# Attention scores on one Trainium2 core: the low part of the queries against 64 rows of the keys, two heads side by side

## The chip, the cores and the metric

The kernel is written instruction by instruction for one core of one Trainium2 chip. The metric is device microseconds of one execution; a run of the kernel is timed several times and the median is given. The engines of the core are TensorE (PE; its weight loads are listed as PEld), VectorE (DVE), ScalarE (ACT), GpSimd (POOL) and SyncE (SP, which here only issues DMAs). Each engine executes its own queue in order, and they wait for one another by semaphores.

## The reference, cut to what matters

One layer of a streaming encoder over 2048 prompt tokens and 32 tokens of a running stream with 1024 cached keys: a projection, a convolution group, an attention group, an output projection, and a mixture of experts. The change touches the scores of the attention group (8 heads of 64, query and key normalised, strictly causal, "stick-breaking" weights in place of a softmax):

```
z = einsum('bqhd,bkhd->bhqk', q, k) * 64 ** -0.5
valid = k_pos[None, :] < q_pos[:, None]
log_keep = where(valid, log_sigmoid(-z), 0.0)
later = cumsum(log_keep, axis=3, reverse=True) - log_keep
a = where(valid, exp(log_sigmoid(z) + later), 0.0)
o = einsum('bhqk,bkhd->bqhd', a, v)
```

## The kernel before, in words

The program has three phases with a barrier between them: `phase_project` (norm, input projection, convolution), `phase_attend` (attention, output projection, routing) and `phase_moe` (the experts). The change is in `phase_attend`.

**Precision.** The scores are made from parts. A query is split into an upper part `q_hi`, rounded to the matmul's fp32r type, and the remainder `q_lo`; a key likewise. A head has 64 dimensions and the array 128 rows, so the query parts lie twice in a tile, in rows 0 to 63 and again in rows 64 to 127 (`q_hi` and `q_lo`, each `[128, 2, 4, 128]`: two query tiles in turn, 4 heads of a group, 128 queries). The keys' tile `kt_sb` (`[128, 4, slots * 128]`) has for an even head the upper part in rows 0 to 63 and the lower in rows 64 to 127, and for an odd head the other way round. One matmul over all 128 rows thus gives the query part times upper plus lower key. A score needs two such passes, `q_hi` (line 1292) and `q_lo` (line 1296), summed in a bank of PSUM. So all four products of the parts are in it, lower query times lower key among them.

**Units.** Attention goes through 34 query tiles (two groups of 4 heads, 17 tiles of 128 queries each), and for each through pairs of heads and stretches of up to 4 key tiles of 128, from the latest keys back. One unit is one query tile, one pair of neighbouring heads (an even and an odd one) and one stretch: `attention_units` lists 172, of which 86 have 4 key tiles (512 columns), 70 have 3, 10 have 2 and 6 have 1. In a tile's first stretch, where the causal edge lies (68 units), a bf16 matmul of an identity with a mask adds -1e30 above the diagonal for each head (line 1294).

**Order on PE**, for each step s (the loop at the end of the function for `block.tensor`): `scores(s)`; jobs that `ahead(s)` names; `transpose_weights(s - 3)` (line 1304, up to 8 transposes of 128*128); the rest of the step's jobs; `values(s - 4)` (line 1321, up to 8 matmuls, which take 64 columns of the array per head, the even head into the lower and the odd into the upper half of the partitions of the output). The jobs are the transposes of keys and queries (lines 1230, 1235), the output projection in 12 matmuls of 512 columns (line 1256), transposes for the output and the router; a planner (`attention_jobs`) places up to two or three of them in a step, by due times and a cost count of columns.

**What scores feed.** For unit u ACT first makes `keep` of both heads (line 1413), a sigmoid of the negated scores, then `wgt` of both heads (line 1418), the sigmoid of the scores, both read from the scores' bank. DVE runs a product scan over `keep` for each head (line 1592, into `past`), POOL multiplies `wgt` by `past` (line 1709), PE transposes the result three steps later, ACT and DVE copy it out of PSUM (lines 1426 and 1604), and the values follow one step behind.

**Banks and waits.** Scores have 3 banks of 512 (`zp`), taken in turn, head by head: head number n = 2u + x uses bank n % 3. Before head n's first pass PE waits until `sig_done` tells that the second activation of head n - 3 has read the bank. After its last pass each head raises `z_done`, for which ACT's `keep` of that head waits. DVE also does the keys' and queries' lower parts (lines 1531, 1536) and the output projection's sum (line 1548).

Of the kernel before, what the change touches and what calls it, by code (L numbers as in the profile page):

```python
# [16 lines left out]
P = 128  # L17
# [4 lines left out]
NH, HD = 8, 64  # L22
# [738 lines left out]
def key_count(t):  # L761
    return t + 1 if t < PT else NPK


def key_slot(g, kt):

    if kt >= PT:
        return PT - NPK + kt - PT
    return PT + kt if g == 1 and kt < 4 else kt


def key_tiles(t, lo, hi):
    return [PT + a if t == PT else a for a in range(lo, hi)]
# [119 lines left out]
def phase_attend(nc, io, scr, picks):  # L893


    with ExitStack() as ctx:
        def sb(name, shape, dt=F32):
            return ctx.enter_context(nc.sbuf_tensor("p2_" + name, shape, dt))

        def ps(name, shape):  # L900
            return ctx.enter_context(nc.psum_tensor("p2_" + name, shape, F32))
# [3 lines left out]
        def sem(name):  # L905
            sems.append(nc.alloc_semaphore("p2_" + name))
            return sems[-1]
# [4 lines left out]
        NW, NK, NP, NA, NZ = 4, 2, 3, 4, 3  # L912
        HW = MAXU * P
        UW = PAIR * HW
        kt_sb = sb("kt", [P, HG, NS * P], F32R)
# [4 lines left out]
        q_lo = sb("q_lo", [P, 2, HG, P], F32R)  # L920
# [42 lines left out]
        zp = ps("zp", [P, NZ, 4 * P])  # L963
# [10 lines left out]
        z_done, keep_done, sig_done = sem("z_done"), sem("keep_done"), sem("sig_done")  # L974
# [65 lines left out]
        for u in range(len(units)):  # L1040
            s = u + 3
            w = (units[s][3] - units[s][2]) if s < len(units) else 0
# [20 lines left out]
        def width(u):  # L1063

            return (units[u][3] - units[u][2]) * P
# [133 lines left out]
        def _(pe):  # L1199
# [80 lines left out]
            def scores(u):  # L1280

                i, heads, lo, hi, _ = units[u]
                g, t = TILES[i]
                w, slot = width(u), key_slot(g, key_tiles(t, lo, hi)[0])
                pe.wait_ge(q_done, i + 1)
                pe.wait_ge(k_done, 2 * max(k_at[g, kt] for kt in key_tiles(t, lo, hi)) + 2)
                for x, h in enumerate(heads):
                    n = 2 * u + x
                    if n >= NZ:
                        pe.wait_ge(sig_done, n - NZ + 1)  # L1290
                    dst, mine = zp[:, n % NZ, 0:w], kt_sb[:, h, slot * P:slot * P + w]
                    pe.matmul(dst, q_hi[:, i % 2, h, :], mine, start=True, stop=False)
                    if hi == key_count(t):
                        pe.matmul(zp[:, n % NZ, w - P:w], identb[:, :], mask[:, :], start=False, stop=False,
                                  skip_group_check=True)
                    pe.matmul(dst, q_lo[:, i % 2, h, :], mine, start=False, stop=True).then_inc(z_done, 1)  # L1296

            def transpose_weights(u):
                pe.wait_ge(a_done, u + 1)
# [31 lines left out]
            for s in range(steps):  # L1331
                if s < len(units):
                    scores(s)
                for j in ahead(s):
                    job(j)
                if 0 <= s - 3 < len(units):
                    transpose_weights(s - 3)
                for j in behind(s):
                    job(j)
                if 0 <= s - 4 < len(units):  # L1340
                    values(s - 4)
# [885 lines left out]
```

## Time and profile before

| | |
|---|---|
| median of 3 runs | 2382.69 us (2379.04 to 2384.85) |
| the profiled execution | 2385.66 us, span of its instructions 2383.9 us |
| PE busy | 2175.3 us (91%) |
| PE weight loads (PEld) busy | 1809.6 us (76%) |
| DVE busy | 1823.2 us (76%) |
| ACT busy | 1336.5 us (56%) |
| POOL busy | 822.3 us (34%) |
| granted TensorE clock, mean | 0.962 of full |

Attention takes the stretch from about 549 to 1391 us of the span. A busy share counts the time in which at least one instruction of the engine was under way, and a matmul's record includes its way through the array: records of neighbouring matmuls overlap, so for the cost of one the starts of two neighbours are compared. "issue" as a releaser means that the engine stood idle while the profile shows nothing that it waited for.

### The profile page before, as it was taken

To read this page: it belongs to the slowest core of one execution; us is meant where nothing else is said; L and a number is where in the kernel's file an instruction comes from. 1 tells how busy PE (TensorE), PEld (TensorE's weight loads), DVE (VectorE), ACT (ScalarE), POOL (GpSimd) and SP (SyncE) were. 2 spreads that over 40 slices of the span, in tenths; PEclk is the share of its full clock that TensorE was granted. 3 is DMA by queue.
4 is the path that set the end of the run, shared out by engine and by line. 5 is a ranking of instruction groups with operands and counts; after the bars stand their busy time and mean duration, and the time that the engine had idled before them with its cause. 6 is when DMAs were issued, how large, how long until landed. Compare 5 with 4: busy or idle time off the path is not lost. (4 is left out here: it accounts for less than half of the span.)

```text
span 2383.9 us, 40219 instructions
## 1 busy us (share of the span) xinstructions
PE 2175.3 (91%) x13338; PEld 1809.6 (76%) x13339; DVE 1823.2 (76%) x2345; ACT 1336.5 (56%) x2487; POOL 822.3 (34%) x683
## 2 busy tenths in 40 slices
PE   8999999975989998899999774999999999999997
PEld 6888888854767776687777663888888888888886
DVE  4798999966888898878797856868688646656644
ACT  5223433345766677666666532667687646556633
POOL 0110664652666575555454430111111111111111
PEclk9999999996999999899999886999999999999999
DMA  6543243335332232333221115989899868768852
GB/s 220 194 144 112 97 133 115 112 104 165 103 101 92 68 129 76 86 106 118 80 76 63 45 47 207 359 286 369 290 371 373 275 216 270 256 189 278 278 181 44
DMA packets 210590, 407.03 MB, mean 171 GB/s; under 512 B 51967, under 2 KB 78463, under 8 KB 210461
## 3 DMA queue, kind: packets, MB, share of 16 engines
q1 hardware_dynamic: 196925, 356.11, 42.6%
q0 software_dynamic: 13536, 49.29, 8.9%
q8 instruction: 71, 1.16, 0.2%
q14 instruction: 58, 0.48, 0.1%
HBM read 312.66 MB, written 92.67 MB: 170 GB/s over the span
## 5 line engine op out<-in xcount | busy, mean ns | idle before, releaser
L2062 DVE TENSOR_TENSOR p_w_lo<-p_raw,p_w_hi 128x1024 fp32r<-128x1024 f32 x384 | 446.0, 1219 | 178.5 <-ACT p_w_hi L1864 174.9
L1709 POOL TENSOR_TENSOR p_wgt<-p_wgt,p_past 128x768 f32<-128x768 f32 (+3 forms) x172 | 335.0, 1948 | 362.5 <-DVE p_past L1592 358.4
L1864 ACT ACTIVATE p_w_hi<-p_raw 128x1024 fp32r<-128x1024 f32 x384 | 376.9, 1050 | 63.4 <-PE p_up L1950 51.8
L563 DVE SCALAR_TENSOR_TENSOR p_ut<-p_ut,p_cw 128x512 f32<-128x512 f32 (+1 forms) x480 | 347.8, 799 | 0.0
L1592 DVE TENSOR_TENSOR_SCAN p_past<-p_keep,p_past 128x513 f32<-128x513 f32 (+1 forms) x208 | 304.0, 1501 | 46.3 <-ACT p_keep L1413 45.0
L298 PE MATMUL p_pj<-p_w_hi,p_xt_hi 128*128 128x512 f32 x680 | 271.4, 399 | 7.0 <-DVE p_xt_lo L539 2.4
L298 PE MATMUL p_pj<-p_w_hi,p_xt_lo 128*128 128x512 f32 x680 | 266.7, 392 | 0.0
L298 PE MATMUL p_pj<-p_w_lo,p_xt_hi 128*128 128x512 f32 x680 | 266.1, 391 | 0.0
L1413 ACT ACTIVATE p_keep<-p_zp 128x384 f32<-128x384 f32 (+3 forms) x344 | 168.1, 542 | 134.8 <-PE p_zp L1296 126.9
L1950 PE MATMUL p_gp<-p_w_lo,p_xt_hi 128*128 128x256 f32 x736 | 206.8, 281 | 0.0
L1950 PE MATMUL p_gp<-p_w_hi,p_xt_lo 128*128 128x256 f32 x736 | 206.8, 281 | 0.0
L1950 PE MATMUL p_gp<-p_w_hi,p_xt_hi 128*128 128x256 f32 x736 | 206.7, 281 | 0.0
L1426 ACT ACTIVATE p_at<-p_tp 128x512 f32<-128x512 f32 (+3 forms) x281 | 142.3, 556 | 95.4 <-PE p_tp L1304 95.0
L1592 DVE TENSOR_TENSOR_SCAN p_past<-p_keep 128x385 f32<-128x385 f32 (+3 forms) x136 | 167.2, 1269 | 34.2 <-ACT p_keep L1413 33.5
L1304 PE MATMUL p_tp<-p_ident,p_wgt 128*128 128x128 f32 x1160 | 164.0, 280 | 17.1 <-DVE p_at L1604 16.3
L2136 POOL DMA_INDIRECT y_out<-p_yo,p_at_s x47 | 75.5, 1605 | 288.7 <-ACT p_yo L1893 288.5
L1939 PE MATMUL p_dp<-p_w_hi,p_ht_hi 128*128 128x512 f32 x368 | 152.9, 415 | 20.7 <-DVE p_ht_lo L2083 20.7
L1321 PE MATMUL p_op<-p_at,p_v 128*64 128x128 f32 x2320 | 168.5, 285 | 0.0
L1418 ACT ACTIVATE p_wgt<-p_zp 128x384 f32<-128x384 f32 (+3 forms) x344 | 167.1, 555 | 0.0
L1304 PEld LDWEIGHTS p_tp<-p_ident,p_wgt 128*128 128x128 f32 x1160 | 139.4, 145 | 31.2 <-DVE p_at L1604 20.1
L2124 POOL COPY p_at_g<-p_slots 128x1 int32 (+1 forms) x47 | 8.6, 184 | 445.4 <-PE p_xtp L1920 418.6
L298 PEld LDWEIGHTS p_pj<-p_w_hi,p_xt_hi 128*128 128x128 f32 x680 | 128.5, 189 | 34.4 <-DVE p_xt_lo L539 2.8
(253 smaller groups left out, 5014.4 us busy)
## 6 DMA issues: line engine op xcount, KB each, us to landing
p_raw<-in_w_up SPq DMA_DIRECT2D x128, 512.0 KB, 8.6
p_raw<-in_w_gate SPq DMA_DIRECT2D x128, 512.0 KB, 5.2
p_raw<-in_w_down SPq DMA_DIRECT2D x128, 512.0 KB, 7.1
p_w_raw<-in_w_in SPq DMA_DIRECT2D x40, 256.0 KB, 3.9
p_x<-in_x SPq DMA_DIRECT2D x17, 512.0 KB, 4.3
p_qd<-scr_q SPq DMA_DIRECT2D x68, 128.0 KB, 3.3
p_y<-in_x SPq DMA_DIRECT2D x17, 512.0 KB
scr_y<-p_y SPq DMA_DIRECT2D x17, 512.0 KB, 3.0
```

The source lines that it names most:

```text
L298: last = pe.matmul(pj[:, n % NPJ, :], xa[:, b, k, :], wa[:, place[c], k, :], start=(m == 0), stop=(m == 3 * KT - 1))
L563: dve.scalar_tensor_tensor(dst, src, cw[:, a, j:j + 1], dst, ALU.mult, ALU.add).then_inc(tap_done, 1)
L1304: end = pe.transpose(tp[:, x, b * P:(b + 1) * P], wgt[:, u % NW, x * HW + b * P:x * HW + (b + 1) * P], ident[:, :])
L1321: end = pe.matmul(op[x * HD:(x + 1) * HD, pair * P:(pair + 1) * P], v_sb[:, key_slot(g, kt), h * HD:(h + 1) * HD], at[:, (2 * u + x) % NA, ...
L1413: act.activation(keep_rows[:, u % NK, x, HW - w:HW], zp[:, (2 * u + x) % NZ, 0:w], ACT.Sigmoid, scale=-SCALE).then_inc(keep_done, 1)
L1418: act.activation(wgt[:, u % NW, x * HW:x * HW + w], zp[:, (2 * u + x) % NZ, 0:w], ACT.Sigmoid, scale=SCALE).then_inc(sig_done, 1)
L1592: end = dve.tensor_tensor_scan(past[:, u % NP, to + w + 1:to:-1], src, src, past[:, (u - 1) % NP, to + 1:to + 2] if more else 1.0, ALU.mul ...
L1709: pool.tensor_tensor(mine, mine, past_rows[:, u % NP, :, 2:2 + w], ALU.mult).then_inc(a_done, 1)
L1864: act.activation(w_hi[:, p, :], raw[:, n % RING, :], ACT.Copy).then_inc(whi_done, 1)
L1939: last = pe.matmul(dp[:, c, :], ha[:, f, :], wa[:, KT + f, c * 512:(c + 1) * 512], start=(start and n == 0), stop=(not start and n == 5))
L1950: last = pe.matmul(dst, xa[:, k, :], wa[:, piece, at + lo:at + hi], start=(n == 0), stop=(n == 3 * KT - 1))
L2062: dve.tensor_tensor(w_lo[:, p, :], raw[:, n % RING, :], w_hi[:, p, :].bitcast(F32), ALU.subtract).then_inc(wlo_done, 1)
```

## The change

The two `q_lo` passes of a unit leave the loop over the heads and follow in a loop of their own behind it. Each takes 64 rows in place of 128: rows 0 to 63 for the even head (x = 0), rows 64 to 127 for the odd one (x = 1), which are the rows with the upper part of that head's keys. The product of the lower query part with the lower key part is left out. The order on PE becomes q_hi of the first head, its mask if there is one, q_hi of the second head (behind its wait for the bank), its mask, q_lo of the first, q_lo of the second. Each q_lo still raises `z_done` once.

```diff
@@ -1293,7 +1293,11 @@
                     if hi == key_count(t):
                         pe.matmul(zp[:, n % NZ, w - P:w], identb[:, :], mask[:, :], start=False, stop=False,
                                   skip_group_check=True)
-                    pe.matmul(dst, q_lo[:, i % 2, h, :], mine, start=False, stop=True).then_inc(z_done, 1)
+                for x, h in enumerate(heads):
+
+                    rows = slice(x * HD, (x + 1) * HD)
+                    pe.matmul(zp[:, (2 * u + x) % NZ, 0:w], q_lo[rows, i % 2, h, :],
+                              kt_sb[rows, h, slot * P:slot * P + w], start=False, stop=True).then_inc(z_done, 1)
```

## Rows read from the trace of the kernel before

**Rows 1.** The score lines 1292 and 1294: count, duration min/median/max in ns, first and last start, shapes.
```profile
L1292 PE MATMUL p_zp<-p_kt,p_q_hi x344: 273/401/796, 548.9 to 1389.6; 128*128 128x512 f32 x86, 128*128 128x384 f32 x70, 128*128 128x256 f32 x10, 128*128 128x128 f32 x6
...
L1294 PE MATMUL p_zp<-p_mask,p_identb x136: 229/230/330, 549.1 to 1377.4; 128*128 128x128 bf16 x136
```
**Rows 2.** Busy time of each engine by stretch of attention, in us (number of instructions).
```profile
core 0: us, PE busy (x) PEld busy (x) DVE busy (x) ACT busy (x) POOL busy (x), PEclk, DMA share, GB/s
...
700.00:850.00 150.00, 138.95 (x1058) 110.23 (x1058) 130.02 (x112) 101.53 (x229) 93.06 (x65) 0.98 0.28 88
850.00:1000.00 150.00, 129.05 (x996) 100.62 (x995) 134.04 (x135) 106.24 (x246) 89.59 (x55) 0.95 0.32 98
...
sum 830.00, PE 749.63 PEld 598.62 DVE 701.34 ACT 558.46 POOL 462.02; mean PE 124.94 PEld 99.77 DVE 116.89 ACT 93.08 POOL 77.00
```
**Rows 3.** Waits, 560 to 1390 us: us in total, times, longest.
```profile
ACT p_keep L1413 <- PE p_zp L1296: 126.8, 100, 7.8
...
DVE p_past L1592 <- ACT p_keep L1413: 78.5, 60, 4.4
PEld p_op L1321 <- issue: 31.2, 158, 0.4
PEld p_zp L1292 <- issue: 29.4, 166, 0.3
...
PE p_tp L1304 <- DVE p_at L1604: 16.3, 10, 2.9
...
PE p_zp L1292 <- ACT p_wgt L1418: 3.4, 3, 1.7
```
**Rows 4.** Timeline of PE, 805.7 to 806.7 us: start, duration, instruction.
```profile
805.76 0.39 PE L1256 MATMUL p_mp<-p_wo_lo,p_m_hi 128*128 128x512 f32 x1
805.99 0.40 PE L1256 MATMUL p_mp<-p_wo_hi,p_m_lo 128*128 128x512 f32 x1
806.32 0.65 PE L1321 MATMUL p_op<-p_at,p_v 128*64 128x128 f32 x7
```
**Rows 5.** Timeline of PEld, 17.4 to 18.8 us (first phase).
```profile
17.91 0.32 PEld L306 LDWEIGHTS p_pm<-p_ident,p_sq 30*128 30x128 f32 x4 [0.17 <-issue]
```
**Rows 6.** Timeline of PE, 807.0 to 810.3 us: a unit of 384 columns without a mask.
```profile
807.35 0.45 PE L1292 MATMUL p_zp<-p_kt,p_q_hi 128*128 128x384 f32 x1
807.63 0.34 PE L1296 MATMUL p_zp<-p_kt,p_q_lo 128*128 128x384 f32 x1
807.80 0.35 PE L1292 MATMUL p_zp<-p_kt,p_q_hi 128*128 128x384 f32 x1
807.99 0.34 PE L1296 MATMUL p_zp<-p_kt,p_q_lo 128*128 128x384 f32 x1
808.16 1.04 PE L1304 MATMUL p_tp<-p_ident,p_wgt 128*128 128x128 f32 x8
809.13 1.09 PE L1321 MATMUL p_op<-p_at,p_v 128*64 128x128 f32 x16
```
**Rows 7.** Timeline of PEld, the same stretch.
```profile
807.99 0.97 PEld L1304 LDWEIGHTS p_tp<-p_ident,p_wgt 128*128 128x128 f32 x8
809.13 0.85 PEld L1321 LDWEIGHTS p_op<-p_at,p_v 128*64 128x64 f32 x16 [0.17 <-issue]
```
**Rows 8.** Timeline of PE, 1180.7 to 1182.2 us: a unit of 512 columns without a mask.
```profile
1181.11 0.50 PE L1292 MATMUL p_zp<-p_kt,p_q_hi 128*128 128x512 f32 x1
1181.44 0.39 PE L1296 MATMUL p_zp<-p_kt,p_q_lo 128*128 128x512 f32 x1
1181.67 0.40 PE L1292 MATMUL p_zp<-p_kt,p_q_hi 128*128 128x512 f32 x1
1181.90 0.40 PE L1296 MATMUL p_zp<-p_kt,p_q_lo 128*128 128x512 f32 x1
1182.14 0.27 PE L1304 MATMUL p_tp<-p_ident,p_wgt 128*128 128x128 f32 x1
```
**Rows 9.** Timeline of PE, 1190.3 to 1192.3 us: a unit of 512 columns with masks.
```profile
1190.61 0.50 PE L1292 MATMUL p_zp<-p_kt,p_q_hi 128*128 128x512 f32 x1
1190.96 0.23 PE L1294 MATMUL p_zp<-p_mask,p_identb 128*128 128x128 bf16 x1
...
1191.90 0.60 PE L1263 MATMUL p_mp<-p_ident,p_h 128*128 128x128 f32 x4
```

## The prediction

> **What bounds the kernel now.** Only the attention phase issues the edited lines, from 549 to 1390 us of the span [rows 1]. I read first the busy times by stretch, then the waits of that stretch, then single units on the timeline.
>
> The kernel's three phases follow one another, so time lost or won inside attention is not hidden by the others: the question is whether TensorE (PE) is what attention waits for. Over 560 to 1390 us PE is busy 749.63 of 830.00 us and VectorE (DVE) 701.34 [rows 2]. PE is thus without work for 80.4 us, a tenth: 11 of 150 us from 700 to 850, 21 from 850 to 1000. The waits say the same from the other side: DVE stands 78.5 us in front of its scan until ScalarE (ACT) has made the keep weights, in 60 pieces, and ACT's own wait for the scores is 126.8 us; PE's largest single wait, for a copy of DVE's, is 16.3 us [rows 3]. So attention is paced by PE nine tenths of the time, with DVE close behind.
>
> PE also has idle that no other engine causes: before the values' first weight load 158 times, 31.2 us, and before the scores' first one 166 times, 29.4 us, both put down to "issue", 0.18 to 0.20 us each [rows 3]. They stand where PE goes from full 128*128 matmuls to the 128*64 ones of the values, and back. After a full matmul of 512 columns the next full one begins 0.23 us later (805.76 to 805.99), but the values behind it 0.33 us later (805.99 to 806.32) [rows 4]. So at a change of the array's division the next weight load waits until the array is empty, 0.10 us over the pitch, and then is itself exposed. The four 30*30 matmuls of the first phase, which have fewer rows as well as fewer columns, show the same 0.17 us of held-back load [rows 5].
>
> The Trainium skill has this as a rule (TensorEngine Tiling (Array Packing), Key Properties): a change of tiling mode, not of tile alone, drains TensorE. Rows 3 to 5 agree for columns, and for rows and columns together; no row shows a change of rows alone.
>
> **The change, part by part.** (a) Each head's second pass (q_lo) takes 64 rows instead of 128. (b) The two q_lo passes of a unit move behind both q_hi passes, next to each other, one on the lower 64 rows, one on the upper. The number of instructions, the banks and the semaphore increments stay. They are moved on PE's queue alone, past nothing but the other head's q_hi and mask; no DMA, and nothing of SP or POOL. There are 172 units: 86 with 512 columns, 70 with 384, 10 with 256, 6 with 128 (two heads each, so 344 q_hi passes); 136 masks are 68 units [rows 1].
>
> *Fewer rows, by themselves: nothing.* Full passes cost by columns, 0.23 us at 512 [rows 4] and 0.17 to 0.19 at 384 [rows 6]; no row has 64 rows. I take no gain from (a) alone; only running side by side can give one.
>
> *Running side by side: likely.* The values of the two heads already do it in two column halves: 16 of them take 1.09 us, hardly more than 8 full transposes at 1.04 [rows 6], and their 16 weight loads take 0.85 against 0.97 for 8 [rows 7]. Two halves load and stream in one period. I take the same for row halves: the pair costs one pass. The bounds are one pass (0.23 us at 512) and two.
>
> *Two new changes of division in each unit* (128 rows to 64 and back), besides the two that are there. In an unmasked unit of 512 columns the first q_hi starts at 1181.11, the transposes behind the scores at 1182.14: 1.03 us in steps of 0.33, 0.23, 0.23, 0.24 [rows 8]; the first is 0.10 longer because its weight load is exposed. After the change: 0.33 to the second q_hi; 0.33 until the load of the low pair may start [rows 4]; 0.10 for that exposed load; 0.33 from the pair's stream to the next load; some 0.05 for the transposes' exposed load (half, since a transpose's pitch is about half of a 512 pass; an estimate). Sum 1.14: **0.11 us more** for each of 86 units, 9.5 us.
>
> At 384 columns the unit takes 807.35 to 808.16, 0.81 us [rows 6]. After: 0.28 + 0.28 + 0.10 + 0.28 + 0.05 = 0.99, where the drained steps are 0.33 less the 0.05 by which this pitch is shorter. **0.18 us more** for 70 units, 12.6 us: the saved pass is worth less here and the drains cost the same. The 16 smaller units I put at 0.2 us, 3.2 us. A masked 512 unit takes 1.29 us (1190.61 to 1191.90) [rows 9]; each mask stays behind its q_hi. By the same sum it comes out 0.02 us better than an unmasked one, which I neglect. **PE: 9.5 + 12.6 + 3.2 = 25 us more.**
>
> Bounds of the unknown: without any drain at a change of rows, the pair saves one pitch in each unit, 86 x 0.23 + 86 x 0.18 = 35 us less. With drains and no overlap it is 25 + 35 = 60 us more. With drains and overlap of streams alone, the loads one after the other, it is 172 x 0.10 = 17 us over the forecast. I take 25, since the column halves are the nearest row.
>
> *The moved q_lo delays the first head's scores.* They end now 0.33 + 0.39 = 0.72 us after the first q_hi starts [rows 8]; then 0.33 + 0.33 + 0.10 + 0.39 = 1.15. The second head's end stays (0.33 + 0.23 + 0.23 + 0.40 = 1.19 before). So the first keep activation and the first scan of a unit come 0.43 us later wherever ACT and DVE stand waiting: 60 times, 26 us of more DVE idle at most. PE's being three units ahead of the transposes that need the result hides it, and DVE has 830 - 701 = 129 us without work; with that cover gone it would cost up to those 26 us. I count 0, and it widens the range upward. Also, the second q_hi waits for the bank that the previous unit's activation frees, and now the first q_lo, then the transposes and values, stand behind it. Waits of this kind are 3.4 us now [rows 3]; I add as much again, 3 us.
>
> **Sum.** Of 25 + 3 us nine tenths are on the path (PE is without work a tenth of the time, and takes up delays there): 25 us, less about 2 for stretches where DVE is behind anyway: 23 us. The profiled execution took 2385.66 us (span 2383.9), 3 us over the median of 2382.69; so 2383 + 23 = **2406 us**, 1.0% slower.
>
> The Trainium skill also has a rule that promises a gain (TensorE: Matmul & The Clock Gate, Part 3): matmuls in different row groups run at once, their starts some 4 ns apart. Taken alone it would give the 35 us less of the bounds; no run shows row halves yet.
>
> **The rivals.**
> 1. *No drain for row halves* (faster). The halves' weights load behind the running q_hi, as those of full passes do. For: the column side of the array does not change, and all drained cases in the trace change it. Against: these are all the changes of division there are, and each is drained. Price: 35 us less of PE; DVE (701 us busy) then becomes the bound more often and lets perhaps 0.7 through: 25 us less, **2358**. It decides once the low pair starts less than about 0.25 us behind the second q_hi.
> 2. *Drains, no overlap*: 60 us of PE, nine tenths through, **2438**. For: nothing in the trace shows two row halves at once. Against: rows 6 and 7. That the change does not do what it says lies here too: the passes would run one after the other as full ones do.
> 3. *Small drains, or absorbed*: each drain costs about half of its 0.10; then a 512 unit gains 0.01 and a 384 one 0.08, 6 to 7 us in all; or PE's tenth of idle and DVE's pace take up most of the 25: **2386**.
>
> **How the numbers follow.** Forecast 0.47, rival 1 0.19, rival 2 0.14, rival 3 0.20. A difference of 0.3%, 7 us, is about what a measurement of this kernel can tell from none; 0.17 of rival 3 lies within it, 0.02 above, 0.01 below. Faster 0.19 + 0.01 = 0.20, same 0.17, slower 0.47 + 0.14 + 0.02 = 0.63. Given the forecast alone, 2394 to 2424 (0.07 to 0.24 us a unit). The range reaches from near rival 1 to rival 2, 2362 to 2440, and leaves out about half of the first and a third of the second.
>
> **What would show it.** Right: in a 512 unit the first low pass starts 0.3 us or more behind the second q_hi, with an "issue" idle before its load, and the second low pass within some 0.01 us of the first; the load behind the pair also shows "issue" idle, and these waits grow by some 60 us in total (344 x 0.17); attention ends about 23 us later, and the expert phase keeps its length. Wrong: no new "issue" waits and a low pair that follows in 0.23 us (rival 1); low passes a full pass apart (rival 2); PE's added time there, but its waits for DVE smaller by as much (rival 3).

## The result, and the profile after

The changed kernel takes 2407.3 us (median of 5 runs, 2401.62 to 2411.56) against 2382.69 us before: ratio 1.0099, 95% interval 1.0074 to 1.0124, 24.6 us or 1.0% slower. The forecast was 2406. The profiled execution took 2402.61 us, 5 us under the median; that of before 3 us over its own, so the two traces lie 17 us apart.

The scores' lines in the changed kernel, with the columns of [rows 1]; the idle in front of them and who waited for them:
```profile
L1299 PEld LDWEIGHTS p_zp<-p_kt,p_q_lo x344: 182/183/288, 546.5 to 1406.5; 64*128 64x128 f32 x172
L1299 PE MATMUL p_zp<-p_kt,p_q_lo x344: 322/491/795, 546.5 to 1406.5; 64*128 64x512 f32 x86, 64*128 64x384 f32 x70, 64*128 64x256 f32 x10, 64*128 64x128 f32 x6
...
  issue: 35.4, 104
who waited for it (us, times):
  ACT p_keep L1417: 172.1, 114
```
The scores run from 545.5 us (line 1292's first) to 1406.5, 861 us against 841 before; from the last scores to the end it is 994 us in both. The whole difference lies in attention.

One unit of 512 columns on PE's timeline (739.1 to 740.8 us), then one of 384 (615.8 to 617.1):
```profile
739.28 0.73 PE L1292 MATMUL p_zp<-p_kt,p_q_hi 128*128 128x512 f32 x2
739.95 0.49 PE L1299 MATMUL p_zp<-p_kt,p_q_lo 64*128 64x512 f32 x2
740.37 0.65 PE L1308 MATMUL p_tp<-p_ident,p_wgt 128*128 128x128 f32 x4
...
615.91 0.62 PE L1292 MATMUL p_zp<-p_kt,p_q_hi 128*128 128x384 f32 x2
616.45 0.44 PE L1299 MATMUL p_zp<-p_kt,p_q_lo 64*128 64x384 f32 x2
616.82 0.55 PE L1308 MATMUL p_tp<-p_ident,p_wgt 128*128 128x128 f32 x3
```
The two low passes take 0.49 us together; each alone would be 0.49 as well (0.39 plus the exposed load), so they run at the same time. (A matmul's record begins with its own exposed load: 0.50 us instead of 0.40.) The pair starts 0.67 us behind the first q_hi (forecast 0.33 + 0.33) and the transposes 0.42 behind the pair (0.10 + 0.33). With the transposes' exposed load (0.05: four of them last 0.65 us here and 0.60 in e1, which has no drain there) the unit of 512 takes 1.14 us, as forecast, and that of 384 0.96 (0.99 forecast), against 1.03 and 0.81 in [rows 8] and [rows 6]. PEld's timeline of another 512 unit (1193.0 to 1195.0 us) shows both drains as "issue":
```profile
1193.33 0.30 PEld L1292 LDWEIGHTS p_zp<-p_kt,p_q_hi 128*128 128x128 f32 x2 [0.17 <-issue]
1193.99 0.19 PEld L1299 LDWEIGHTS p_zp<-p_kt,p_q_lo 64*128 64x128 f32 x2 [0.37 <-issue]
1194.42 0.64 PEld L1308 LDWEIGHTS p_tp<-p_ident,p_wgt 128*128 128x128 f32 x6 [0.25 <-issue]
```
The waits and the busy times of the changed kernel from 560 to 1390 us, to be read beside [rows 3] and [rows 2]:
```profile
ACT p_keep L1417 <- PE p_zp L1299: 169.1, 110, 7.7
DVE p_past L1596 <- ACT p_keep L1417: 103.1, 72, 5.1
PEld p_zp L1299 <- issue: 34.3, 101, 0.7
...
PEld p_tp L1308 <- issue: 13.3, 57, 0.9
```
```profile
sum 830.00, PE 756.62 PEld 562.89 DVE 675.99 ACT 543.85 POOL 451.46; mean PE 126.10 PEld 93.82 DVE 112.66 ACT 90.64 POOL 75.24
```
Two things stand here side by side. PE is busier and has two new drains. But DVE's wait for the first activations has grown by 25 us (78.5 to 103.1), more than the 17 us between the two traces. The busy times of this window must be read with care: the changed kernel's attention goes on for 17 us more behind 1390 us, and that work is missing in its row. So PE is 7 us busier in the window but 25 us over the whole execution (2175.3 to 2200.3), and DVE 25 us less busy in the window but 14 over the whole (1823.2 to 1809.0). The forecast put the loss on PE's time and counted the delay at nothing. The experiments had to part them.

### The profile page after: what moved, and what is told of

Read it like the earlier page. It is cut to its first block and busy times, and to the rows that moved or that the text cites. A ratio compares the mean times of both kernels' runs of the same rounds, so it can differ in the third digit from the quotient of the medians.

```text
span 2400.9 us, 40219 instructions
## 1 busy us (share of the span) xinstructions
PE 2200.3 (92%) x13338; PEld 1787.3 (74%) x13339; DVE 1809.0 (75%) x2345; ACT 1336.1 (56%) x2487; POOL 824.6 (34%) x683
## 3 DMA queue, kind: packets, MB, share of 16 engines
q8 instruction: 71, 1.16, 0.2%
## 5 line engine op out<-in xcount | busy, mean ns | idle before, releaser
L1596 DVE TENSOR_TENSOR_SCAN p_past<-p_keep,p_past 128x513 f32<-128x513 f32 (+1 forms) x208 | 296.4, 1464 | 67.7 <-ACT p_keep L1417 63.4
L1596 DVE TENSOR_TENSOR_SCAN p_past<-p_keep 128x385 f32<-128x385 f32 (+3 forms) x136 | 162.1, 1232 | 47.2 <-ACT p_keep L1417 44.9
L1308 PE MATMUL p_tp<-p_ident,p_wgt 128*128 128x128 f32 x1160 | 169.7, 286 | 16.2 <-DVE p_at L1608 15.1
L1325 PEld LDWEIGHTS p_op<-p_at,p_v 128*64 128x64 f32 x2320 | 129.9, 142 | 33.4 <-issue 32.6
```

The costliest lines, as they stand in the source:

```text
L1308: end = pe.transpose(tp[:, x, b * P:(b + 1) * P], wgt[:, u % NW, x * HW + b * P:x * HW + (b + 1) * P], ident[:, :])
L1325: end = pe.matmul(op[x * HD:(x + 1) * HD, pair * P:(pair + 1) * P], v_sb[:, key_slot(g, kt), h * HD:(h + 1) * HD], at[:, (2 * u + x) % NA, ...
L1596: end = dve.tensor_tensor_scan(past[:, u % NP, to + w + 1:to:-1], src, src, past[:, (u - 1) % NP, to + 1:to + 2] if more else 1.0, ALU.mul ...
```

## The experiments

They ran on three chips, each time beside the kernel before, whose medians there were 2382.09 us (e1 to e4), 2382.34 (e5 to e8) and 2383.03 (e9 to e11). By "theory" the expectations mean the one held at that time. "Delay" is how much later than before the first head's scores of an unmasked 512-column unit end, counted from the start of its first q_hi (0.72 us before, 1.16 in the changed kernel: delay 0.44).

**e1: the order alone.** Both q_lo behind both q_hi, all over 128 rows.
```diff
-                    pe.matmul(dst, q_lo[:, i % 2, h, :], mine, start=False, stop=True).then_inc(z_done, 1)
+                for x, h in enumerate(heads):
+                    pe.matmul(zp[:, (2 * u + x) % NZ, 0:w], q_lo[:, i % 2, h, :],
+                              kt_sb[:, h, slot * P:slot * P + w], start=False, stop=True).then_inc(z_done, 1)
```


> The order of the change, but both q_lo passes over all 128 rows: no change of division, no halves side by side. Drain theory (the added time is PE's, from two more drained changes of division in each unit, and the later scores of the first head cost nothing): PE's time for a unit is that of before, so 2380 to 2388 us, no measurable difference from before; the first head's scores still come about 0.47 us later (0.33 + 0.23 + 0.23 + 0.39 against 0.33 + 0.39) and DVE's wait in front of the scan grows from 78.5 us as it did in the changed kernel (108.3). Rival (the delay is what costs: DVE gets a unit's first scan late and PE later waits for DVE): most of the 24.6 us are here too, 2398 to 2408 us.

Measured: 2392.35 us, ratio 1.0036 (1.0024 to 1.0049), 10.3 us slower: between the two. PE's unit on the timeline (737.2 to 738.8 us) and DVE's wait, 560 to 1390 us:
```profile
737.42 0.73 PE L1292 MATMUL p_zp<-p_kt,p_q_hi 128*128 128x512 f32 x2
737.99 0.63 PE L1297 MATMUL p_zp<-p_kt,p_q_lo 128*128 128x512 f32 x2
738.46 0.60 PE L1306 MATMUL p_tp<-p_ident,p_wgt 128*128 128x128 f32 x4
```
```profile
DVE p_past L1594 <- ACT p_keep L1415: 96.9, 67, 3.3
```
The unit takes PE 1.04 us, as before (1.03), and still the kernel is slower, with 18 us more of DVE's wait. My 0.47 us of delay was wrong: the first q_lo starts 0.57 us in and ends at 0.96, a delay of 0.24.

**e2: 64 rows in the old order**, four new changes of division in each unit.
```diff
-                    pe.matmul(dst, q_lo[:, i % 2, h, :], mine, start=False, stop=True).then_inc(z_done, 1)
+                    rows = slice(x * HD, (x + 1) * HD)
+                    pe.matmul(dst, q_lo[rows, i % 2, h, :], kt_sb[rows, h, slot * P:slot * P + w],
+                              start=False, stop=True).then_inc(z_done, 1)
```


> 64 rows, but in the order of before (q_hi, q_lo of the first head, q_hi, q_lo of the second): four new changes of division in each unit instead of two, and nothing side by side. Drain theory: at 512 columns 4 x 0.10 exposed load + 4 x 0.33 to the next load + 0.05 = 1.77 us against 1.03 before; at 384 columns 4 x 0.10 + 4 x 0.27 + 0.05 = 1.53 against 0.81: 0.72 to 0.74 us more for each of 172 units, 125 us of PE, nine tenths of it through: about 2498 us (2485 to 2512). If drains cost nothing and 64 rows were slow for another reason (each pass 0.1 us longer), 344 x 0.1 = 34 us: about 2415. Late-scores rival: the first head's scores come earlier than in the changed kernel, 0.33 + 0.33 + 0.10 + 0.39 minus one q_hi step, so it would be faster than 2407.

Measured: 2439.31 us, ratio 1.0243 (1.0225 to 1.0261), 57 us slower instead of 115. A unit of 512 columns on PE (743.4 to 745.6 us), and the busy times from 560 to 1390:
```profile
743.54 0.50 PE L1293 MATMUL p_zp<-p_kt,p_q_hi 128*128 128x512 f32 x1
743.97 0.50 PE L1297 MATMUL p_zp<-p_kt,p_q_lo 64*128 64x512 f32 x1
744.40 0.50 PE L1293 MATMUL p_zp<-p_kt,p_q_hi 128*128 128x512 f32 x1
744.83 0.49 PE L1297 MATMUL p_zp<-p_kt,p_q_lo 64*128 64x512 f32 x1
745.25 0.55 PE L1306 MATMUL p_tp<-p_ident,p_wgt 128*128 128x128 f32 x3
```
```profile
sum 830.00, PE 803.76 PEld 578.05 DVE 611.88 ACT 539.12 POOL 424.03; mean PE 803.76 PEld 578.05 DVE 611.88 ACT 539.12 POOL 424.03
```
Every step is 0.42 to 0.43 = 0.33 + 0.10: the drain's price is confirmed to the hundredth, 1.71 + 0.05 against 1.03 us a unit, 125 us in all. But only 57 come through, 0.46 of it: PE's time without work in this window falls from 80 to 26 us. The "nine tenths" of the forecast is refuted. So is the rival that late scores are the only cost, which expected less than 2407 us. The 57 are not PE's time alone either: the first head's scores end at 0.43 + 0.50 = 0.93 us, a delay of 0.21.

**e3: both low passes on the same row half.** Against the changed kernel:
```diff
-                    rows = slice(x * HD, (x + 1) * HD)
+                    rows = slice(0, HD)
```

> The order of the change with both q_lo passes on rows 0 to 63, so that they use one and the same row half. (The odd head then gets its lower query part times the lower part of the key instead of the upper one.) Two changes of division as in the changed kernel, but nothing can run side by side. If running side by side is what holds the loss down: the second q_lo starts a pass (0.23 us at 512 columns, 0.18 at 384) behind the first instead of 0.003 us, 35 us more of PE than in the changed kernel, about 0.93 of it through: 2440 us (2430 to 2448). If the two halves gain nothing by being different: 2407 us.

Measured: 2416.67 us, ratio 1.0138 (1.0121 to 1.0156), 34.6 us over the kernel before. The changed kernel, run again as e8 on another chip, is 24.1 over its own, so the same row half costs some 10 us instead of 33. On the timeline (739.2 to 740.8 us):
```profile
739.28 0.73 PE L1292 MATMUL p_zp<-p_kt,p_q_hi 128*128 128x512 f32 x2
739.95 0.73 PE L1298 MATMUL p_zp<-p_kt,p_q_lo 64*128 64x512 f32 x2
740.61 0.44 PE L1307 MATMUL p_tp<-p_ident,p_wgt 128*128 128x128 f32 x2
```
The pair now takes 0.73 us instead of 0.49. Side by side does save a pass (0.24 us here, some 34 us of PE in all), but a microsecond of PE's time is worth only 0.3 in the result (10 of 34), where the first head's scores come no later than in the changed kernel.

**e4: the low pair first**, behind the values, so that only one new change of division is left.
```diff
-                    dst, mine = zp[:, n % NZ, 0:w], kt_sb[:, h, slot * P:slot * P + w]
-                    pe.matmul(dst, q_hi[:, i % 2, h, :], mine, start=True, stop=False)
+                    rows = slice(x * HD, (x + 1) * HD)
+                    pe.matmul(zp[:, n % NZ, 0:w], q_lo[rows, i % 2, h, :],
+                              kt_sb[rows, h, slot * P:slot * P + w], start=True, stop=False)
+                for x, h in enumerate(heads):
+                    n = 2 * u + x
                     if hi == key_count(t):
                         pe.matmul(zp[:, n % NZ, w - P:w], identb[:, :], mask[:, :], start=False, stop=False,
                                   skip_group_check=True)
-                    pe.matmul(dst, q_lo[:, i % 2, h, :], mine, start=False, stop=True).then_inc(z_done, 1)
+                    pe.matmul(zp[:, n % NZ, 0:w], q_hi[:, i % 2, h, :], kt_sb[:, h, slot * P:slot * P + w],
+                              start=False, stop=True).then_inc(z_done, 1)
```


> The two 64-row passes side by side at the head of the unit, right behind the values' matmuls of the unit before, then both full q_hi passes. The change from the values to the scores is drained anyway, so only one new change of division is left in a unit. Drain theory: at 512 columns 0.10 + 0.33 + 0.10 + 0.23 + 0.23 = 0.99 us against 1.03 before, at 384 columns 0.10 + 0.27 + 0.10 + 0.18 + 0.18 = 0.83 against 0.81: 86 x -0.04 + 70 x 0.02 + 16 x 0.03 = -2 us of PE, so 2378 to 2388 us, no measurable difference from before and some 24 us under the changed kernel. Rival (64-row passes or their order cost in themselves, wherever they stand): 2395 us or more. Late-scores rival: the first head's scores end at 0.10 + 0.33 + 0.10 + 0.39 = 0.92 us instead of 0.72 before and 1.15 in the changed kernel, so about half of the loss, 2395 us.

Measured: 2389.67 us, ratio 1.0030 (1.0020 to 1.0041), 7.6 us slower: over the 2378 to 2388 of the drains alone, under the 2395 of both rivals. On the timeline (737.7 to 739.1 us):
```profile
737.80 0.50 PE L1292 MATMUL p_zp<-p_kt,p_q_lo 64*128 64x512 f32 x2
738.24 0.73 PE L1299 MATMUL p_zp<-p_kt,p_q_hi 128*128 128x512 f32 x2
738.80 0.49 PE L1308 MATMUL p_tp<-p_ident,p_wgt 128*128 128x128 f32 x3
```
1.00 us, 0.03 less than before, and yet slower. The first head ends at 0.44 + 0.10 + 0.39 = 0.93: a delay of 0.21. Next to e1 (0.24 and 10.3 us) this pointed at the delay, so the next run made nothing but a delay.

**e5: only the signal late.** PE's program is that of before; ACT waits for both heads before it starts on the first.
```diff
-                    act.wait_ge(z_done, 2 * u + x + 1)
+                    act.wait_ge(z_done, 2 * u + 2)
```


> The kernel before, with PE's instructions all as they were; only ACT's keep activation of the first head also waits for the second head's scores (z_done of 2u + 2 instead of 2u + 1). So the first head's keep comes about 0.47 us later, as in e1, and nothing else changes: no other order of the passes, no other place of the wait for the bank. Theory (e1's 10 us are the price of the first head's late scores, through ACT and DVE): the same as e1, 2388 to 2396 us, with DVE's wait in front of the scan near 99 us. Rival (e1's 10 us come from the order on PE, the first q_lo standing behind the second q_hi's wait for its bank): 2380 to 2385 us, as before.

Measured: 2401.38 us, ratio 1.0083 (1.0069 to 1.0097), **19.0 us slower with not one PE instruction changed**. DVE's wait:
```profile
DVE p_past L1592 <- ACT p_keep L1413: 104.7, 67, 5.1
```
This is the changed kernel's wait (103.1). I had expected e1's 10 us, by the wrong delay for e1; with the right ones, 0.24 us make 10.3 and 0.46 us (0.33 + 0.23 + 0.23 + 0.39 less 0.72) make 19.0: 43 and 41 us of result for each us of delay. Those are the delays of unmasked 512-column units; read in the same way for every unit and averaged, they are 0.25 us in e1, 0.45 in e5 and 0.42 in the changed kernel, so the price stays at 41 to 43. The rival, that e1's loss came from the q_lo's place behind the bank's wait, is not needed. What this run does not show is the way by which the delay costs: the granted clock is lower as well, 0.956 to 0.958 where all but two of the 19 runs of the kernel before beside it have 0.961 to 0.963. The clock is taken up behind e11.

**e6: PE's time taken away.** The 104 unmasked units have no q_lo passes at all.
```diff
-                    pe.matmul(dst, q_hi[:, i % 2, h, :], mine, start=True, stop=False)
-                    if hi == key_count(t):
+                    masked = hi == key_count(t)
+                    end = pe.matmul(dst, q_hi[:, i % 2, h, :], mine, start=True, stop=not masked)
+                    if masked:
...
-                    pe.matmul(dst, q_lo[:, i % 2, h, :], mine, start=False, stop=True).then_inc(z_done, 1)
+                        end = pe.matmul(dst, q_lo[:, i % 2, h, :], mine, start=False, stop=True)
+                    end.then_inc(z_done, 1)
```

> The kernel before without the q_lo passes in the 104 units that have no mask (the product of the lower query part with the whole key is left out there). This measures how much of PE time saved comes out of the result, which is what rival 1 (no drain) would have brought. PE is spared 140 passes of 0.23 and 68 of 0.18 us, 44 us, and both heads' scores come earlier. If PE alone set the pace: nine tenths, 40 us, 2342 us. Theory after e1 to e3 (only about half of PE's time is passed on, since e2's 119 us of PE made 57): about 20 us, 2362 us (2355 to 2370).

Measured: 2376.98 us, ratio 0.9977 (0.9967 to 0.9987), only 5.4 us faster for 44 us of PE, outside the expected 2355 to 2370. These units' first heads end 0.23 us earlier (0.18 at 384 columns); over 172 units that is 0.13, which at 41 us for each us gives 5.3 by itself. But the run does not show that PE's time is worth nothing. The granted clock was 0.952 to 0.956 here, and in the profiled execution this took up to 21 us of PE's full-speed time more than before (the table behind e11). So of the 44 us spared up to half went back into a slower PE. That rival 1 would have brought 25 us is refuted all the same: more PE time than its 35 us, taken away together with a part of the delay, brings 5.

**e7: low pair first in masked units alone.**
```diff
+                if hi == key_count(t):
...
+                    return
```
with e4's two loops between these lines, and the old loop without its mask behind them.

> A candidate for a better kernel: the two 64-row passes side by side at the head of the unit, but only in the 68 units with a mask, where e4's units were 0.08 (384 columns) to 0.14 us (512) shorter than before; the other 104 units as before. PE: 36 x 0.08 + 16 x 0.14 + 16 x 0.03 = 5.6 us less; about half passed on, less what later first scores cost: 2377 to 2383 us, at most 0.2% under before. Rival (64-row passes cost in themselves): 2386 us or more.

Measured: 2386.32 us, ratio 1.0022 (1.0012 to 1.0032): 4.0 us slower, though PE has less to do. The masked units' first heads end some 0.09 us later than before, over all units 0.04, which makes 1.5 us by the price above; the rest is not explained.

**e8: the changed kernel again.**

> The changed kernel again, on the same chip and beside the same runs of the kernel before as e5 to e7, as a base for them: 2403 to 2411 us, ratio 1.009 to 1.011.

Measured: 2406.42 us, ratio 1.0100 (1.0085 to 1.0116).

**e9: the scores one place ahead.** If late scores are the price, earlier scores must pay, in the kernel before as in the changed one.
```diff
             for s in range(steps):
-                if s < len(units):
-                    scores(s)
                 for j in ahead(s):
                     job(j)
...
                 for j in behind(s):
                     job(j)
+                if s + 1 < len(units):
+                    scores(s + 1)
                 if 0 <= s - 4 < len(units):
                     values(s - 4)
```
(with `scores(0)` ahead of the loop.)

> The kernel before with its full passes, but PE issues the scores of unit s + 1 ahead of the values of unit s - 4 instead of behind them; nothing else moves. The number of changes of division stays (transposes to scores is none, scores to values one, values to transposes one). A unit's scores come earlier by about the time of its values, up to 1.1 us; the values come later by the time of the scores. Theory (after e1, e5 and e6: the pace is set by how late the scores reach ACT and DVE, about 41 us for each us of delay, and hardly by PE's own time): DVE's wait in front of the scan, 78.5 us in 60 pieces of 1.3 us on average, shrinks clearly, and the kernel gets 10 to 35 us faster, 2347 to 2372 us. Rival (PE's time sets the pace): no difference, 2378 to 2386 us. Against it: the wait of the second head for its bank now also holds up the values; if that decides, 2390 us or more.

Measured: 2377.11 us, ratio 0.9974 (0.9962 to 0.9986), 5.9 us faster. DVE's wait for keep falls from 78.5 to
```profile
DVE p_past L1593 <- ACT p_keep L1414: 54.1, 54, 3.9
```
The direction is right, the size under the expected 10, 2377.11 being just outside both expected ranges: the second head's wait for its bank appears more often, and now holds up the values, as at 741.39 us:
```profile
741.39 0.44 PE L1292 MATMUL p_zp<-p_kt,p_q_hi 128*128 128x384 f32 x1 [0.51 <-ACT p_wgt L1419]
```
**e10: the same in the changed kernel.**

> The same swap in the changed kernel. The change from the 64-row passes to the values is then the only drained one behind the scores, so the unit has one new change of division instead of two; in PE's time that is about even with e9 (-0.03 us at 512 columns, +0.02 at 384). The first head's scores still come 0.33 us later than in e9. Theory: with the scores issued earlier, fewer units wait for them, so the loss against e9 is a good deal under the 24.6 us: 0 to 12 us. If it is still 20 us or more, the loss does not come from late scores.

Measured: 2379.14 us, ratio to the kernel before 0.9989 (0.9974 to 1.0004). Against e9 the change now costs 2.0 us instead of 24.6. That is not the delay's cover alone: the low pair now stands next to the values, so one of its two drains falls on a change that is there anyway, and PE's busy time is about that of e9 (743.38 us in the window from 560 to 1390 against 746.65). It is e11, without a change on PE, that shows how much of the delay is covered.
```profile
DVE p_past L1597 <- ACT p_keep L1418: 60.8, 56, 3.9
```
**e11: e9 with the late signal of e5.**

> e9 with the late signal of e5 (ACT's keep of the first head also waits for the second head's scores; PE's instructions as in e9). Theory: with the scores ahead the delay of 0.46 us costs less than the 19 us of e5: 3 to 14 us over e9. If it costs 19 us or more again, issuing the scores earlier did not cover any of it.

Measured: 2380.45 us, ratio 0.9986 (0.9975 to 0.9997): 3.3 us over e9, where the same delay cost 19.0 in the old place.

The lowest ratio of all is e9's, 0.26% under the kernel before.

**The granted clock beside these runs.** A mean clock c over a span T takes at most (1 - c) x T of PE's full-speed time. An estimate for the profiled executions:

| run | clock | (1 - clock) x span, us | against before | the median's change |
|---|---|---|---|---|
| before | 0.962 | 91 | | |
| e1 | 0.958 | 101 | +10 | +10.3 |
| e5 | 0.957 | 103 | +13 | +19.0 |
| changed | 0.957 | 103 | +13 | +24.6 |
| e4 | 0.955 | 108 | +17 | +7.6 |
| e6 | 0.953 | 112 | +21 | -5.4 |
| e2 | 0.965 | 85 | -5 | +57.2 |
| e9 | 0.962 | 90 | 0 | -5.9 |

```profile
560.00:1390.00 830.00, 749.63 (x5632) 598.62 (x5630) 701.34 (x801) 558.46 (x1274) 462.02 (x318) 0.96 0.28 88
560.00:1390.00 830.00, 742.75 (x5480) 591.55 (x5479) 678.02 (x787) 544.08 (x1247) 452.71 (x314) 0.94 0.28 87
560.00:1390.00 830.00, 728.61 (x5469) 575.00 (x5470) 706.42 (x803) 558.16 (x1273) 472.03 (x323) 0.93 0.28 87
560.00:1390.00 830.00, 803.76 (x5301) 578.05 (x5302) 611.88 (x756) 539.12 (x1205) 424.03 (x303) 0.97 0.27 85
```
(before, e5, e6 and e2, with the columns of [rows 2]; the third number from the end is the clock.) In e5 and e6, where PE is idle for longer, the clock is lower, in e2, where it is idle for less, higher; the changed kernel, 756.62 us busy at 0.94, does not fit by its busy time alone. The clock by itself does not order the losses: e4 has a lower one than e5 and loses less, and its delay is the smaller one. But the clock may be a part of the price. So two rivals stand for *how* a delay costs: DVE's wait, or a slower PE in the stretches where the delay opens gaps. At one and the same clock, 0.958, single runs can be compared: e5 took 2400.34 and 2400.67 us and the kernel before beside it 2390.03; the changed kernel (e8) took 2402.27 there and the kernel before, in eight runs on the three chips, 2385.81 to 2390.54. That leaves 10 us of e5's 19 and 12 to 16 of the changed kernel's 24.6 without any help from the clock. The rest may have come by way of it; no run parts the two.

## Why the prediction was right, and where not

**The total** was right, 2406 against 2407.3, but by luck in part: it rested on two wrong terms that made up for one another.

- *The drains*: right in place and size. A change of rows alone drains as one of columns does; 0.33 and 0.10 us appear as forecast. The unit of 512 came out at 1.14 us as summed, that of 384 at 0.96 for 0.99. The new "issue" idle in front of the low pair and of the transposes is 48 us (34.3 + 13.3), with smaller entries before other jobs; forecast some 60. A unit with a mask pays less than an unmasked one, and by more than the 0.02 us that the forecast neglected: the 512-column form goes from 1.29 us [rows 9] to 1.30 + 0.05 (PE, 1203.2 to 1204.7 us, below), 0.06 more instead of 0.11. The mask's weight load is held back less often in the changed kernel, 29 times for 4.7 us instead of 62 times for 11.7. With this PE's added time is some 20 us (an estimate from the medians of each form), where 25 were forecast. The rule on a change of tiling mode (the Trainium skill, TensorEngine Tiling (Array Packing), Key Properties) held here for rows alone too.
```profile
1203.27 0.50 PE L1292 MATMUL p_zp<-p_kt,p_q_hi 128*128 128x512 f32 x1
1203.62 0.23 PE L1294 MATMUL p_zp<-p_mask,p_identb 128*128 128x128 bf16 x1
1203.65 0.48 PE L1292 MATMUL p_zp<-p_kt,p_q_hi 128*128 128x512 f32 x1
1203.98 0.23 PE L1294 MATMUL p_zp<-p_mask,p_identb 128*128 128x128 bf16 x1
1204.13 0.51 PE L1299 MATMUL p_zp<-p_kt,p_q_lo 64*128 64x512 f32 x2
1204.57 0.33 PE L1263 MATMUL p_mp<-p_ident,p_h 128*128 128x128 f32 x1
```
- *A row misread*: "no row shows a change of rows alone" is not so. In [rows 5] the weights loaded are 30 rows by 128 columns, and the matmul uses 30 rows and all 128 columns of the array; only what streams through is 30 wide (PE of the kernel before, at 17.92 us):
```profile
17.92 0.43 PE L306 MATMUL p_pm<-p_ident,p_sq 30*128 30x30 f32 x4
```
  Its load was held back 0.17 us all the same. The trace of the kernel before thus already spoke against rival 1, whose chance of 0.19 was too high, and its "For" (all drained cases change the column side) was wrong.
- *Side by side*: right. The second low pass costs nothing in the changed kernel and 0.24 us in e3. In all 172 units of the changed kernel's trace the second pass starts 3 to 4 ns behind the first.
- *The delay of the first head, "I count 0"*: this step failed. Its size was right (0.43 us forecast, 0.44 found), and the bound beside it, 60 waits of DVE by 0.43 us = 26 us, was near the truth: at 41 us for each us it is 18 of the 24.6 us. The cover named for it was the wrong one. PE's three units ahead cover what PE needs from a scan; they do not cover DVE, which stands idle for this very unit's scores. And DVE's 129 us without work are no slack for it, since 78.5 of them are this wait, which a delay makes longer. That this wait is the way by which the whole of the 18 us comes is not shown: a part may come by the lower clock.
- *"Nine tenths" of PE's time on the path*: this step failed as well. A high busy share of PE and few waits were read as pace. Measured, PE's time is worth about 0.3 (e3: 10 us for 34), next to nothing beyond the delay in e6, where the clock fell too, and at most 0.46 when 125 us are put on (e2). For the change's 20 us or so 0.3 gives 6.
- 18 + 6 = 24 us, against 24.6. That the two add up is an estimate: the delay's share was measured by itself (e5), PE's only through e3.
- *Rival 1's price* was wrong by the same steps: without any drain the order would have been that of e1, whose delay costs 10.3 us, and 35 us less of PE would have brought some 0.3 of it, 10 us. It would have ended between no change and 10 us slower, not 25 us faster (an estimate from e1, e3 and e6, not run).
- *Rival 3* held that DVE's pace and PE's idle would absorb PE's time. About 0.7 of it is absorbed (e3), but the delay came in its place. Whether DVE or the clock absorbs it is not shown: in e3 the clock was 0.958 to 0.960, in the changed kernel 0.955 to 0.958.

What stays open: why each us of delay costs 0.24 us in each of 172 units (41 / 172) and not more or less, how much of that comes by the clock, and most of e7's 4 us.

## What to carry to other kernels

A busy engine with few waits need not set the pace: look at which engine waits for its result, and in how many pieces; a wait in n pieces prices a delay at up to n times the delay (60 pieces before the change, 41 found). When instructions are regrouped for one engine's sake, note for every consumer when its first input is ready, not only how long the group takes. Read the granted clock beside every experiment that gives or takes PE time: here it fell when PE was spared work (e6) and rose when PE was loaded (e2), and either can hide a part of what the experiment asks for. And a change of the array's division was paid at both ends: here the two drains and the exposed loads cost more than the pass they saved, unless the group stands next to a change that is there anyway.

## What the runs showed that I had not expected

- A one-line change of what ACT waits for, with PE's stream as it was, cost 0.8% (e5): a third of what 125 us of added PE time cost (2.4%, e2).
- The time of one and the same program goes with its granted clock: of 14 runs of the kernel before (beside e1 to e4), the three at 0.958 took 2385.81 to 2387.33 us and the six at 0.962 took 2378.63 to 2382.62. In e10 the nine runs at 0.961 and 0.962 took 2375.28 to 2380.84 us and the three at 0.957 took 2386.52 to 2389.65. The changed kernel's runs had 0.955 to 0.958, e2's, with PE nearly without gaps, 0.961 to 0.965. Which is cause and which effect from run to run is not shown.
- A short bf16 matmul between fp32r ones is held back too: before the mask's weight load PEld stood idle with "issue" 62 times for 11.7 us in the kernel before and 66 times for 12.2 us in e9, which keeps its order of the passes, but 30 times for 4.8 us in e1, with both masks among full q_hi passes.
